# Work for the next group of a down projection put between additions, and one more place for arriving weights

## What is computed

```python
x = x + (gates[:, :, 0] * y_a + gates[:, :, 1] * y_b) @ w_out[l]
hc = rmsnorm(x, norm_cross_g[l])
x = x + memory_cross_attention(hc, mem_n, w_xq[l], w_xkv[l], w_xo[l])   # 4 heads of 128
hf = rmsnorm(x, norm_ffn_g[l])
g, u = jnp.split(hf @ w_gu[l], 2, axis=-1)      # 2 x 5632 columns
x = x + (jax.nn.silu(g) * u) @ w_down[l]        # 5632 rows
return rmsnorm(x, final_norm_g)
```

## Time and profile before

| | us |
|---|---|
| median of 3 runs | 2825.31 (2821.89 to 2825.94) |
| profiled execution, own time | 2823.73 |
| its span in the profile | 2821.8 |
| TensorE busy | 2731.7 (97%) |
| VectorE busy | 1717.8 (61%) |
| ScalarE busy | 1018.3 (36%) |
| GpSimd busy | 771.8 (27%) |

### The profile page before, as it was taken

One profiled execution on the slowest core, in us unless ns is written; L12 is line 12 of the kernel. 1 busy time (PEld: TensorE's weight loads), 2 busy tenths in 40 slices (PEclk: granted clock), 3 DMA queues, 4 the chain that ended last, 5 costly groups with the idle time before them and its releaser, 6 DMA issues.

```text
span 2821.8 us, 35057 instructions
## 1 busy us (share of the span) xinstructions
PE 2731.7 (97%) x13710; PEld 2285.7 (81%) x13710; DVE 1717.8 (61%) x1904; ACT 1018.3 (36%) x1134; POOL 771.8 (27%) x642
## 2 busy tenths in 40 slices
PE   9999999999999999999999999999999989999997
PEld 7888888888788888896777888888888877777776
DVE  6667643345633353663767767676767666666666
ACT  6545532225632231343623333333333322222224
POOL 0000000000000003500366666666666621313130
PEclk9999999999999999999999999999999999999999
DMA  6222233332233352342333343434444464343432
GB/s 239 68 89 74 67 101 97 97 97 83 68 97 97 97 187 90 97 150 74 105 125 107 127 134 128 135 128 134 129 133 130 132 224 150 119 149 118 151 116 82
DMA packets 115138, 333.30 MB, mean 118 GB/s; under 512 B 10320, under 2 KB 43088, under 8 KB 114384
## 3 DMA queue, kind: packets, MB, share of 16 engines
q1 hardware_dynamic: 108544, 309.37, 33.8%
q10 hardware_dynamic: 6480, 22.35, 1.9%
HBM read 301.27 MB, written 30.41 MB: 118 GB/s over the span
## 4 chain that ended last, share of the span: by engine, by line
PE 75%; DVE 18%; ACT 3%; issue 3%; DMA 1%; POOL 0%; SPq 0%; DVEq 0%; ACTq 0%
PE acc L1795 14%; PE acc L1797 14%; PE acc L1796 14%; PE ps L2169 9%; PE acc L1822 4%; PE ps L2170 4%; PE acc L1824 4%; PE acc L1823 4%; DVE w_lo L1585 2%; PE acc L2169 2%; DVE cg L1613 2%; DVE cg L1614 2%; DVE cu L1613 2%; DVE cu L1614 2%; DVE w_lo L1098 2%
## 5 line engine op out<-in xcount | busy, mean ns | idle before, releaser
L1098 DVE TENSOR_TENSOR w_lo<-raw,w_hi 128x1024 fp32r<-128x1024 f32 x328 | 456.5, 1397 | 287.1 <-ACT w_hi L610 286.6
L1795 PE MATMUL acc<-act_both,w_hi 128*128 128x512 f32 (+1 forms) x1536 | 591.5, 385 | 5.9 <-DVE w_lo L1098 4.5
L1797 PE MATMUL acc<-act_both,w_lo 128*128 128x512 f32 (+1 forms) x1536 | 585.4, 381 | 0.0
L1796 PE MATMUL acc<-act_both,w_hi 128*128 128x512 f32 (+1 forms) x1536 | 585.2, 381 | 0.0
L610 ACT ACTIVATE w_hi<-raw 128x1024 fp32r<-128x1024 f32 x328 | 344.4, 1054 | 599.0 <-PE acc L1797 343.0
L1795 PEld LDWEIGHTS acc<-act_both,w_hi 128*128 128x128 f32 x1536 | 289.6, 189 | 62.6 <-issue 6.0
L1797 PEld LDWEIGHTS acc<-act_both,w_lo 128*128 128x128 f32 x1536 | 289.4, 188 | 55.6
L1796 PEld LDWEIGHTS acc<-act_both,w_hi 128*128 128x128 f32 x1536 | 289.6, 189 | 54.7 <-issue 0.7
L2169 PE MATMUL ps<-t_both,w_hi 128*128 128x512 f32 x896 | 325.9, 398 | 0.0
L1822 PE MATMUL acc<-act_both,w_hi 128*128 128x512 f32 x672 | 265.5, 395 | 33.9 <-DVE x L1453 27.2
L544 POOL MEMSET mem_stat<- 128x256 f32 x1 | 0.3, 311 | 1048.1 <-DMA mem<-mem_t 1048.1
(11 more groups left out here) (299 smaller groups left out, 4909.8 us busy)
## 6 DMA issues: line engine op xcount, KB each, us to landing
raw<-w_stream SPq DMA_DIRECT2D x440, 512.0 KB, 3.6
over<-w_stream SPq DMA_DIRECT2D x56, 512.0 KB, 4.1
gate_t<-cg ACTq DMA_DIRECT2D x22, 512.0 KB, 2.6
over<-gate_t SPq DMA_DIRECT2D x22, 512.0 KB, 5.0
up_t<-cu ACTq DMA_DIRECT2D x20, 512.0 KB, 2.6
over<-up_t SPq DMA_DIRECT2D x20, 512.0 KB, 6.2
x<-x_t SPq DMA_DIRECT2D x16, 512.0 KB, 8.5
x_tokens<-x_n SPq DMA_DIRECT2D x4, 1024.0 KB, 15.5
```

What stands on the lines that cost most here:

```text
L1098: nc.vector.tensor_tensor(w_lo[:, s, :], raw[:, s, :], f(w_hi[:, s, :]), ALU.subtract)\
L1795: nc.tensor.matmul(dst, wh, ah, start=start and k == 0, stop=False)
L1796: nc.tensor.matmul(dst, wh, al, start=False, stop=False)
L1797: last = nc.tensor.matmul(dst, wl, ah, start=False, stop=stop and k == UK - 1)
```

## The change

Four edits:
- **Down projection.** `down` takes a function `between` that runs between the two additions of a pair. The work for the next group goes there, one operation of 128 x 1024 to a pair: gate multiplications at pairs 1 and 3, up multiplications at 2 and 4, low halves at 5 and 6. ScalarE's sigmoids and high halves go among its conversions to match, and its waits for the last stores move from ahead of all groups into the sigmoid.
- **Cross output projection.** `units()` goes from ahead of the even addition to behind it and the low half that follows.
- **Seam before the mixed products and the one behind them.** VectorE's order changes: a weight low half between the two halves of the mixed activations, the reciprocal behind the first mixed unit; at the last pass one weight low half before the hidden low halves and one inside the last `read_products`. ScalarE's first down conversion goes ahead of the hidden high halves. TensorE asks for the second output's bank after one reading step instead of after the whole reading. The first four down units are issued by SyncE before the transfers of `x`.
- **Four places for arriving mixed units**: the fourth in a free part of `over_hi`. The halves keep three places.

```diff
@@ def mix_raw(n)
-            if n % 3 == 2:
-                return over_lo[:, 0:UK, SH:S]
-            return raw[:, 2 * (n % 3):2 * (n % 3) + 2, :].rearrange("p r (b c) -> p (r b) c", b=4)
+            if n % 4 >= 2:
+                return (over_lo, over_hi)[n % 4 - 2][:, 0:UK, SH:S]
+            return raw[:, 2 * (n % 4):2 * (n % 4) + 2, :].rearrange("p r (b c) -> p (r b) c", b=4)
@@ SyncE
-                else:
-                    sp.wait_ge(lo_done, U_MIX + (-2, 0)[n] if n < 2 else U_MIX + n - 2)
+                elif n != 3:
+                    sp.wait_ge(lo_done, U_MIX + (-2, 0)[n] if n < 2 else U_MIX + n - 3)
...
-                sp.wait_ge(lo_done, U_DOWN - 2 if n < 2 else U_DOWN - 1 if n < 4 else U_DOWN + n - RING + 1)
+                sp.wait_ge(lo_done, U_DOWN - 3 if n < 2 else U_DOWN - 2 if n < 4 else U_DOWN + n - RING + 1)
...
+            for n in range(4):
+                late_weights(n)
             for c in range(4):
                 sp.wait_ge(unit_done, U_DOWN - 3 + c)
                 if c == 1:
                     hidden_in(0)
-                    late_weights(0)
-                    late_weights(1)
-                if c == 2:
-                    late_weights(2)
-                    late_weights(3)
                 x_in_again(c)
@@ ScalarE
+            def sigmoid_high(slot, b):
+                act.wait_ge(gate_stored, 16 * (MIXES + 1))
+                act.wait_ge(up_stored, 16 * (MIXES - INLINE + 1))
+                act.wait_ge(gate_scaled, sig_no.at(1))
+                nc.scalar.activation(sig_tmp(b), over_lo[:, hid_part(slot, b), :], ACT.Sigmoid).then_inc(sig_made, 1)
...
                 if last:
                     mix_convert()
+                    convert(1)
                     act.wait_ge(hid_in[0], 32)
...
-                    convert(1)
                     convert(1)
                     convert(2)
...
             def group(slot):
-                units(3)
-                sigmoids(slot)
-                units(3)
-                hidden_high(slot)
                 units(2)
+                sigmoid_high(slot, 0)
+                units(2)
+                sigmoid_high(slot, 2)
+                units()
+                hidden_high(slot, 0)
+                units()
+                hidden_high(slot, 2)
+                units(2)
@@ VectorE, cross output projection
             for m in range(KT):
-                if m % 2 == 0:
-                    units()
                 dve.wait_ge(half_done if m % 2 == 0 else unit_done, unit.at(1 - (0 if m % 2 else U_XO)))
                 add_out(m)
                 if m:
                     x_low(act_lo[:, m - 1, :], act_hi[:, m - 1, :], m - 1, G_FFN)
                 if m % 2:
                     unit.add()
+                else:
+                    units()
@@ VectorE, read_products(g, dst, between)
                 added(out[:, 3, :], out[:, 2, :], lambda h: half(3, h), freed)
+                between()
                 dve.wait_ge(products_done, len(TOLD) * g + 4)
@@ VectorE, before the mixed products
             mixed_low(0)
-            rstd_of(4, rstd, S)
+            units()
             mixed_low(1)
-            units(2)
+            units()
             unit.add(4 * DIRECT)
             out_no.add(2 * DIRECT)
-            mix_low(5)
+            mix_low()
+            rstd_of(4, rstd, S)
+            mix_low(4)
@@ VectorE, last pass
                 mix_low()
                 if last:
-                    hidden_low(0)
+                    units()
+                    hidden_low(0, 0)
+                    hidden_low(0, 2)
...
-                read_products(2 * p - 1, cu)
+                read_products(2 * p - 1, cu, units if last else lambda: None)
...
                 if last:
-                    units(3)
+                    units()
@@ VectorE, middle(slot, first)
+                def next_group(n):
+                    if n == 1:
+                        dve.wait_ge(hid_in[slot], arrived[slot].at(64))
+                        arrived[slot].add(64)
+                    if n in (1, 3):
+                        times_rstd(over_lo, n - 1, gate_scaled)
+                    elif n in (2, 4):
+                        times_rstd(over_hi, n - 2, up_scaled)
+                    elif n in (5, 6):
+                        hidden_low(slot, 2 * (n - 5))
                 for n in range(KT // 2):
-                    down(2 * n, first=first)
-                    if n == 2:
-                        dve.wait_ge(hid_in[slot], arrived[slot].at(64))
...
-                    if n == 3:
...
-                    if n == 6:
-                        hidden_low(slot)
+                    down(2 * n, first=first, between=lambda: next_group(n))
@@ TensorE
-            down(0, split.at(), banks=(READ_STEPS * (2 * MIXES - 2) + 1, READ_STEPS * 2 * MIXES))
+            down(0, split.at(), banks=(READ_STEPS * (2 * MIXES - 2) + 1, READ_STEPS * (2 * MIXES - 1) + 1))
```

52 lines of the change are left out of this document (20 added, 32 removed).

## The result

The changed kernel takes **2776.35 us** (median of 4 runs, 2774.28 to 2776.82), the kernel before 2823.6 beside it (2821.53 to 2825.94). The ratio is 0.9831, with a 95% interval of 0.9814 to 0.9848. The forecast was 2777.0. The profiled execution took 2776.34 us, with a span of 2774.3, so 47.5 us less span than before.

What follows compares the result with a forecast made beforehand. TensorE, busy 97% of the span, was taken to bound the kernel. Gains of 32 + 3.9 + 6.1 + 4.5 + 2 = 48.5 us from 2823.73 gave 2775.2, with 1.6 to the median 2777; range 2766 to 2796.

Steps and rivals of the forecast that it cites:

- (a): Down projection, ten groups: loss per group falls from 3.41 to about 0.2 us; gain 32 us, bounds 22 and 34.
- (d): Cross output projection: subtraction between a pair's additions, steps from 6.12 to 5.44 us; gain 4.5 us, bounds 3 and 5.
- still covered, barely: Down projection: hidden values landing after 10.2 us, the longest, make the addition 1.9 us late against 1.99 allowed.
- signs of being wrong: Group over 44.5 us, VectorE waiting for arriving hidden values, or mixed products over 20.1 us a step.
- (b): Mixed products to down projection: TensorE's 6.7 us stop becomes 3.8 a pair later; gain 3.9 us, bounds 1 and 7.
- (c): Last units before mixed products: 4.31 us stop and slow clock behind it go; gain 6.1 us, bounds 4.3 and 6.5.
- (e): Mixed products: four places for arriving units remove steps pushed by late transfers; gain 2 us, bounds -3 and 7.
- Rival 1: Down projection: GpSimd's multiplications take 3 us instead of 2.4, collisions overrun; gain there 19, time 2790 us; chance 0.2.
- Rival 2: Mixed products: GpSimd's sums slow the subtractions after each reading, 74 us in all; time 2851 us; chance 0.04.
- my bound of 20.1: Mixed products: the prediction is wrong if they take more than 20.1 us a step.
- Rival 3: Down projection: a group's stops move to pairs 3 and 4 instead of going; time 2809 us; chance 0.07.

Runs made afterwards that it cites:

- the version with both edits: Changed kernel with ScalarE's conversion of pair 4 ahead of the second sigmoid and the first two down additions inside the last reading of products: 2772.6 us.

## Why the prediction was right

**Sum.** 48.5 us predicted, 47.5 measured in the span. That the forecast of 2777.0 was only 0.65 too high is partly luck. By medians the gain was 47.25 us, 1.1 less than I had, and the kernel before ran 1.7 lower beside the changed one (2823.6) than the median from which I started. Within the sum, 1.8 too much in (a) stands against 1.0 too little in (d), which the clock gave.

**(a) Down projection, 30.2 for 32.** The method was right to a few hundredths. Counted from T = 2366.81, I had the first addition of pairs 2, 3, 4 and 5 starting with delays of 1.0, 0.9, 1.86 and 1.77 us; the rows give 0.96 (2375.93), 0.89, 1.85 (2387.70) and 1.77. The steps that made this possible: blocking for whole instructions, the restart 0.73 us after an addition began, and the conversion behind the second sigmoid. Two terms were mis-sized. The cover was 1.79 us and not 1.99: an addition on time already starts 0.20 after the next output has begun (2385.85 against 2385.65), which I had left out. So the cover left at pair 4, 0.13 us by my count, was less than nothing: the next output would have begun at 2388.37 (2388.14 + 0.23) and began at 2388.43, 0.73 after the addition of 2387.70, with slower starts behind it. That costs the 0.2 us of each group which I had put in as a round figure. And "still covered, barely" for the late hidden values was wrong: I looked for their cost at the addition behind the multiplication, where the cover was 0.1 at the longest landing of 10.2. It came out three pairs later, since everything in the group shifts by the delay and the thinnest cover is at pair 4; a landing of 7.7 us sufficed. That is the 1.7 us by which (a) fell short, and two of my signs of being wrong did show, though small: the wait in VectorE's row (1.4 us), and one group over 44.5 us, the first (45.10).

**(b) Seam, 3.8 for 3.9.** The stop of 6.7 before the first matmul became one of 3.81 at the third output, predicted as 3.8, and the clock fell behind it. The first addition came at 2275.20, 9.0 us after the last mixed matmul, and I had it 9.1 after (2288.7 less 2279.6). Two parts of the price were off and cancelled: counted from the last mixed matmul, the third output starts 5.55 us earlier (9.83 against 15.38, where it starts at 2294.99), for 5.8, and the fall of the clock cost 1.7, for 1.9.

**(c) 6.3 for 6.1, (d) 5.5 for 4.5.** In (d) 1.1 us is not the edit's: when the stage begins, the clock is still low, and this costs 1.3 us in the kernel before and 0.3 in the changed one. In other runs of the same code the stage takes 44.2 to 45.5 us, the more the longer the clock is low. The other 4.4 are the edit's, near the 4.5 summed. My picture of the loop lacked GpSimd's blocking (0.79 us in each subtraction); the sum did not need it, since I took the step from the rows.

**(e) 1.5 for 2**, in one pair of traces; by the runs unresolved. In the steady part of that pair the gain is 2.2 (723.5 against 721.2), but the fourth place alone did not show it.

**The rivals.** Rival 1 (2790) fell because GpSimd's multiplications took 2.40 us, as I had written, and not 3. My working gave a little less, 2.25 us (2412.19 less 2409.94). Rival 2's collisions did not come: steady mixed steps were 20.04 us, under my bound of 20.1. Rival 3 named the right place, pair 4, but there a delay of 1.85 us stood against a cover of 1.79. The test without GpSimd's work bears out how the old loss was shared: 1.57 blocking, 1.84 order.

## What to carry to other kernels

Where one engine is full and the others serve it through two banks, count for each release how late it may come (bank period less restart time, less what an addition on time already starts behind the next output: 2.72 - 0.73 - 0.20 = 1.79 us here), and spread foreign work so that no interval holds more than one operation and one collision; that turned 3.41 us a group into 0.2. A cover must be followed to the thinnest place of the whole cycle, not only to the next release: a delay of 0.76 us was free for three pairs and cost 0.55 at the fourth. And put the conversion that the critical engine needs ahead of work that waits for someone else, in every queue; at a seam, list all transfers in flight before moving any one of them.

## What the runs showed of the hardware

- **How often the clock falls.** There are 14 profiled kernels, one execution each. In the first two passes of mixed products, with stops of 2.4 to 3.4 us at two or three places, the clock fell to 1.2 GHz for 3.4 us (1.7 us lost) once in twelve of them, twice in one, and in one once and then once more for 6.9 us. Behind the stop near 1510 or 1520 alone it stayed at 2.4 GHz in seven kernels, fell in six and stayed low twice as long in one. It fell in all after stops of 3.78 us and more, and at the seam after 2.37 and 2.29 us but not after 2.18. From 1400 to the end of the down projection it never fell after a stop of 1.75 us or less, and after stops of 1.83 to 1.88 us it fell in three cases of eight.
- **What a fall costs.** Up to the 1.7 us, and less where a later stop takes it up. In the kernel before it fell behind the stop of 1.83 us at 2735.74, and the second stop of that group, 1.10 us, is missing; with the fourth place alone there is no fall there, the stop of 1.10 is there, and the stretch from the second pair to the final norm is only 0.4 us shorter. The time of a run follows its mean granted clock: in 15 runs of the kernel before, those at 0.991 took 2828.75 and 2828.84 us, those at 0.993 2823.86 to 2827.44, at 0.994 2822.45 to 2823.72 and at 0.995 2820.26 and 2821.86.
- **Blocking costs nearly the whole own time.** A VectorE subtraction that meets GpSimd's 2.40 us instruction ends 1.1 us after it (2376.01 against 2374.93), so 2.58 us where it alone takes 1.23; additions with one operand in PSUM took 0.67 to 0.69 us beside GpSimd and alone.
- **Full DMA engines.** At a share of 1.0 (405 GB/s from 2272 to 2290 in the version with both edits) a 512 KB unit took 13.2 us to land and a store 7.3, where their medians are 3.6 and 2.6.
- **Smaller packets at the same mean.** The fourth place is a tile split into rows of 1 KB: 84 units instead of 56 land in such places, and the packets rise from 115138 to 125890 for the same 333.3 MB. Over all mixed units the landing has a median of 4.1 us in both kernels. But with three places both kinds of places show it (4.1 and 4.1), and with four the split ones have 4.7 and the others 3.6. Why was not tested.
